# First attention of a two-block transformer kernel: late heads turned in every other pair, compressed branch one pair later

## What is computed

```
q = (rms_norm(to_heads(q, 16), q_gain) * 64 ** -0.5)
kc = rms_norm(compress_blocks(to_heads(kc, g), ...), k_gain[0])      # 15 compressed keys
s_c = einsum(qc, kc) - slopes * dist_c
p_c = masked_softmax(s_c, dist_c >= 0);  o_c = einsum(p_c, vc)
s_s, s_w = scores on the selected and on the window keys;  o_s, o_w = softmax(...) @ v
o = gc[..., 0:1] * o_c + gc[..., 1:2] * o_s + gc[..., 2:3] * o_w
```

## Time and profile before

| | |
|---|---|
| median of 3 runs | 1295.48 us (1290.08 to 1297.04) |
| the profiled execution | 1299.4 us, of which 1297.4 us span |
| TensorE (matmul) busy | 1225.7 us, 94% |
| VectorE busy | 965.9 us, 74% |
| ScalarE busy | 777.4 us, 60% |
| the first attention's loop | about 95 to 169.20 us of the span, where the out-projection's first product starts |
| one weight chunk | 1024.0 KB, 5.3 us from issue to landing |
| mean granted TensorE clock | 0.982 |

### The profile page before, as it was taken

The page is one execution under the profiler, slowest core; times in us unless marked ns, Lnnn a source line. Parts: engine busy times, 40 slices in busy tenths (PEclk is TensorE's granted clock), DMA queues, the critical chain, the costliest instruction groups (busy, mean ns, idle before and its releaser), DMA issues.

```text
span 1297.4 us, 15596 instructions
## 1 busy us (share of the span) xinstructions
PE 1225.7 (94%) x5843; PEld 1000.4 (77%) x5843; DVE 965.9 (74%) x1341; ACT 777.4 (60%) x1155; POOL 20.2 (2%) x36
## 2 busy tenths in 40 slices
PE   7998999999999998999999998999997989999997
PEld 5887777888887786788788776877876867788886
DVE  4978848898987887569989876778786865575545
ACT  6566736677777677557767667433446565543443
POOL 0000000000000000000000000000000001000000
PEclk9998999999999999999999999999999989999999
DMA  7660114798995512429999836777775713467420
GB/s 314 259 240 1 65 66 155 302 367 352 352 364 210 220 58 69 179 103 371 371 344 370 343 106 229 293 310 282 284 306 204 312 61 115 145 279 290 177 98 33
DMA packets 41466, 291.84 MB, mean 225 GB/s; under 512 B 4736, under 2 KB 5120, under 8 KB 6576
## 3 DMA queue, kind: packets, MB, share of 16 engines
q1 hardware_dynamic: 40464, 287.82, 57.9%
q0 software_dynamic: 784, 2.63, 0.7%
q10 hardware_dynamic: 144, 0.39, 0.1%
HBM read 289.78 MB, written 1.05 MB: 224 GB/s over the span
## 4 chain that ended last, share of the span: by engine, by line
PE 67%; DVE 15%; ACT 9%; issue 4%; DMA 4%; POOL 0%; DVEq 0%; ACTq 0%; POOLq 0%
PE ps L422 18%; PE ps L424 18%; PE ps L423 18%; DVE wl L1609 5%; ACT wh L1148 4%; DMA ring<-stream_dram 4%; DVE AR L1833 3%; PE ps L606 2%; ACT AR L1257 1%; PE ps L961 1%; ACT XN L1160 1%; PE ps L559 1%; PE ps L450 1%; PE ps L607 1%; DMA AR<-kr_dram 1%
## 5 line engine op out<-in xcount | busy, mean ns | idle before, releaser
L1609 DVE TENSOR_TENSOR wl<-ring,wh 128x2048 fp32r<-128x2048 f32 x229 | 526.4, 2302 | 165.8 <-ACT wh L1148 162.2
L1148 ACT ACTIVATE wh<-ring 128x2048 fp32r<-128x2048 f32 x232 | 443.8, 1914 | 147.9 <-PE ps L424 80.7
L422 PE MATMUL ps<-wh,XH 128*128 128x512 f32 x1040 | 419.1, 403 | 9.9 <-DVE XH L1653 4.1
L424 PE MATMUL ps<-wh,XL 128*128 128x512 f32 x1040 | 408.1, 392 | 0.0
L423 PE MATMUL ps<-wl,XH 128*128 128x512 f32 x1040 | 407.3, 392 | 0.0
L422 PEld LDWEIGHTS ps<-wh,XH 128*128 128x128 f32 x1040 | 196.9, 189 | 56.5 <-issue 9.9
L424 PEld LDWEIGHTS ps<-wh,XL 128*128 128x128 f32 x1040 | 196.5, 189 | 43.1
L423 PEld LDWEIGHTS ps<-wl,XH 128*128 128x128 f32 x1040 | 197.4, 190 | 38.1 <-issue 0.7
L422 PE MATMUL ps<-wh,HT 128*128 128x512 f32 x360 | 142.6, 396 | 4.0 <-DVE HT L2004 2.9
L424 PE MATMUL ps<-wh,HT 128*128 128x512 f32 x360 | 140.8, 391 | 0.0
L423 PE MATMUL ps<-wl,HT 128*128 128x512 f32 x360 | 140.6, 390 | 0.0
(11 more groups left out here) (299 smaller groups left out, 1255.3 us busy)
## 6 DMA issues: line engine op xcount, KB each, us to landing
ring<-stream_dram SPq DMA_DIRECT2D x272, 1024.0 KB, 5.3
H<-x_dram SPq DMA_DIRECT2D x2, 512.0 KB, 5.0
out_dram<-XN SPq DMA_DIRECT2D x4, 256.0 KB, 2.0
XN<-ag_dram POOLq DMA_DIRECT2D x1, 768.0 KB, 4.5
AR<-pT_dram POOLq DMA_DIRECT2D x2, 256.0 KB, 2.8
AR<-g_final_dram POOLq DMA_DIRECT2D x1, 512.0 KB, 4.8
C<-cols_dram ACTq DMA_DIRECT2D x1, 385.0 KB, 4.7
ring<-stream_dram SPq DMA_DIRECT2D x2, 144.0 KB, 5.2
```

The lines of the kernel that those rows point to most:

```text
L422: e.matmul(o, ah, bh, start=start, stop=False)
L424: return e.matmul(o, al, bh, start=False, stop=stop)
L1148: e.activation(wh[:, k % WBUF, :], ring[:, n % RING, :], ACT.Copy, scale=1.0).then_inc(up("whi", ("whi", k)))
L1609: e.tensor_tensor(wl[:, k % WBUF, :], ring[:, n % RING, :], h.bitcast(F32), ALU.subtract).then_inc(up("wlo", ("wlo", k)))
```

## The change

Of the eight hooks, the late heads move from steps 1, 2, 3, 4 to steps 1, 3, 5, 7 on all three engines; the last two groups go to the banks 0 to 3 of the scores instead of bank 6. The first half of the compressed branch stays in step 0 on TensorE, but in bank 5 and not in the next of 4 and 5; on VectorE it moves from step 0 to step 1, behind the first group of late heads, on ScalarE from step 1 to step 2; its normalising stays in step 2, its turning in step 3. The second half moves from step 6 to step 8, its normalising from 7 to 9, its turning from 8 to 10. The weight splits move from steps 8 and 11 to 6 and 12.

```diff
--- before.py
+++ after.py
@@ -995,7 +995,7 @@
                 project("q1", "mix0", lambda t: [("qsq", 1, t)], between=second_layer)
 
                 def compressed(hf):
-                    b = bank("cs", hf, by=[("cs", hf)], of=(0, 1, 2, 3) if hf else (4, 5))
+                    b = bank("cs", hf, by=[("cs", hf)], of=(0, 1, 2, 3) if hf else (5,))
                     e.wait_ge(*at("kb"))
                     e.wait_ge(*at("lo", ("qt", hf), 6))
                     for t in range(TT):
@@ -1024,13 +1024,13 @@
                     k = [("lo", ("kt", a), j) for a in range(2) for j in (0, 2)] if i == 0 else []
                     return k + ([("lo", ("qt", i // 8), i % 8)] if i % 2 == 0 else [])
 
-                def late_heads(*js):
-                    turn_heads(("qt", 1), QN[:, :, 512:1024], js, [("qn", 1)], (6,))
+                def late_heads(*js, of=(6,)):
+                    turn_heads(("qt", 1), QN[:, :, 512:1024], js, [("qn", 1)], of)
 
                 attention("nsa", nsa_pairs, keys, 0, ready,
-                          {0: lambda: compressed(0), 1: lambda: late_heads(0, 1), 2: lambda: late_heads(2, 3), 3: lambda: late_heads(4, 5),
-                           4: lambda: late_heads(6, 7), 6: lambda: compressed(1)}, closing,
-                          {3: lambda: turn_compressed(0), 8: lambda: turn_compressed(1)})
+                          {0: lambda: compressed(0), 1: lambda: late_heads(0, 1), 3: lambda: late_heads(2, 3), 5: lambda: late_heads(4, 5, of=(0, 1, 2, 3)),
+                           7: lambda: late_heads(6, 7, of=(0, 1, 2, 3)), 8: lambda: compressed(1)}, closing,
+                          {3: lambda: turn_compressed(0), 10: lambda: turn_compressed(1)})
 
             def moba():
                 project_first("skv", "kv", lambda t: [("skvsq", t)], lambda: key_rows(1), (6, 7))
@@ -1478,12 +1478,8 @@
                 def late_heads(*js):
                     high(("qt", 1), js, lambda j: q_of(8 + j), S[:, 8:9])
 
-                def weigh_and_late():
-                    late_heads(0, 1)
-                    weigh(0)
-
-                attention("nsa", nsa_pairs, 0, {1: weigh_and_late, 2: lambda: late_heads(2, 3), 3: lambda: late_heads(4, 5), 4: lambda: late_heads(6, 7),
-                                                6: lambda: weigh(1)}, (8, 11))
+                attention("nsa", nsa_pairs, 0, {1: lambda: late_heads(0, 1), 2: lambda: weigh(0), 3: lambda: late_heads(2, 3), 5: lambda: late_heads(4, 5),
+                                                7: lambda: late_heads(6, 7), 8: lambda: weigh(1)}, (6, 12))
 
             def moba(stage):
                 def query_rows(t):
@@ -2201,24 +2197,20 @@
                     e.wait_ge(*at("pct_full", hf))
                     e.tensor_copy(PCT[:, 256 * hf:256 * hf + 256], ps("pct", hf)[0:120, 0:256]).then_inc(up("dve", ("pct", hf)))
 
-                def first_hook():
-                    q_norm("qn", "qroot", 1)
+                def second_hook():
+                    late_heads(0, 1)
                     e.wait_ge(*at("ct"))
                     compressed(0)
 
-                def third_hook():
+                def fourth_hook():
                     late_heads(2, 3)
-                    normalise(0)
-
-                def fourth_hook():
-                    late_heads(4, 5)
                     turn_compressed(0)
 
                 compressed_keys()
                 q_part(1)
                 attention("nsa", nsa_pairs, 0, True,
-                          {0: first_hook, 1: lambda: late_heads(0, 1), 2: third_hook, 3: fourth_hook, 4: lambda: late_heads(6, 7),
-                           6: lambda: compressed(1), 7: lambda: normalise(1), 8: lambda: turn_compressed(1)}, (8, 11))
+                          {0: lambda: q_norm("qn", "qroot", 1), 1: second_hook, 2: lambda: normalise(0), 3: fourth_hook, 5: lambda: late_heads(4, 5),
+                           7: lambda: late_heads(6, 7), 8: lambda: compressed(1), 9: lambda: normalise(1), 10: lambda: turn_compressed(1)}, (6, 12))
 
             def moba():
                 take()
```

## The result

The changed kernel took 1302.13 us (median of 12 runs, 1298.88 to 1303.26), the kernel before 1295.28 (12 runs on the same chip, 1290.08 to 1297.20). The ratio is 1.0056, with a 95% interval of 1.0045 to 1.0068. So the sign was right and the size was not: +6.85 us, where the sum said +2.7. The profiled execution took 1303.11 us, its span is 1301.1.

What follows compares the result with a forecast made beforehand. TensorE, busy 94% of the span, was taken to bound the kernel, so only its waits count: 1.0 + 2.15 - 0.5 = 2.65, say +2.7, on 1295.48 gives 1298.2 us; range 1293.0 to 1303.0, 8 in 10.

Steps and rivals of the forecast that it cites:

- the sum: Whole kernel: waits of 1.0 and 2.15 us less 0.5 gained, 2.65, taken as +2.7 us; chance 0.40.
- The first term: First pairs, up to pair 5's scores at 117.5 us: TensorE gains 0.5 us after the waits behind it.
- The clock probably falls here too, as behind the 3.8 us. That costs little: First pairs: lower clock near 106 us costs little, as TensorE waits again, up to 2 us for copies, 0.5 for weights.
- the other bound: First pairs: 0.6 us lost instead of 0.5 gained, if the lower clock lasts beyond 111 us.
- The second and third terms: Pairs 8 and 9: TensorE waits 1.0 us for heads 6, 7, then 2.15 us before turning pair 7.
- Rival 1: Pairs 8 and 9: the clock falls in the new stall and all counts, +4.4 us, 1299.9 us; chance 0.32.
- The rest of the kernel moves along: Behind the stage: everything only shifts by the stage's +2.7 us, with no further gain or loss.
- Five microseconds at half rate cost about 2.5: Kernel before, behind the 3.8 us wait before the second late-head group: clock 0.50 until about 111 us costs about 2.5 us.
- rival 2: Pairs 5 to 9 stall under 0.5 us and the clock stays up near 106 us: about -1.5 us, 1294.0; chance 0.16.
- the bound of 0.5%: Whole kernel: a measurement can tell 0.5%, 6.5 us, from no change; chance of staying within it 0.88.
- A slowing by over 6.5 us: Whole kernel: needs rival 1 and a high run, or two falls of the clock; chance 0.09.

Runs made afterwards that it cites:

- second half another pair on: Changed kernel with the second compressed branch in pair 9 and the weight splits in 8 and 12; 1298.45 us, ratio 1.0027.
- 32 transposes: Kernel before plus 32 transposes whose output nothing reads, behind the whole first attention; 1299.13 us, ratio 1.0024.
- second look at before: Kernel before, unchanged, profiled once more for a second trace; 1294.20 us.
- second look at after: Changed kernel, with no further edit, profiled once more for a second trace; 1303.34 us.
- first branch back: Changed kernel with the first compressed branch back in VectorE's step 0 and its weighing in ScalarE's step 1, bank 5 kept; 1299.45 us, ratio 1.0042.
- splits back: Changed kernel with the two weight splits back in pairs 8 and 11; 1298.86 us, ratio 1.0031.
- both back: Changed kernel with the weight splits back in 8 and 11 and the first compressed branch back in steps 0 and 1; 1296.51 us, ratio 1.0015.
- the kernel with later heads: Kernel before with late heads in steps 3, 4, 6, 7, second branch in 8, splits in 9, 12; 1296.32 us; with transposes filling its waits, 1296.57 us.

## Why the prediction was right and wrong, step by step

| step | forecast | measured |
|---|---|---|
| pair 1's maxima | 100.0 | 100.07 |
| branch on VectorE | 104.9 | 104.81 |
| pair 2's maxima | 106.95 | 106.86 |
| turning of pair 0 waits | 0.8 and 2.6 | 0.57 and 2.20 |
| pair 3's scores | 106.3 | 106.14 |
| waits for copies, weights | 2 and 0.5 | 2.10 and 0.44 |
| pair 3's maxima | 111.4 | 111.26 |
| pair 5's scores | 117.5 | 118.72 |
| pair 7's exponentials | 128.5 | 129.60 |
| products wait for heads 6, 7 | 1.0 | 0.69 |
| pair 8's maxima | 134.5 | 135.51 |
| turning of pair 7 waits | 2.15, to 139.7 | 0.24, to 140.97 |
| end of the stage | 171.8 | 172.80 |

**Up to 111.4 us the queues told it to 0.2 us.** Every time in the first pairs is where three queues, followed in strict order with durations of the kernel before, put it; the two waits of pair 0's turning came 0.2 and 0.4 us shorter than forecast.

**The first term, 0.5 us gained, failed.** The step is "The clock probably falls here too, as behind the 3.8 us. That costs little". It did fall, but not with the long waits: it was still at 1.00 in both and fell at 111.3 us, inside the last short wait (0.44 us, to 111.49), when TensorE had two pairs of work in hand. Pair 5's scores came at 118.72, 1.2 us later than forecast. Against before that is a gain of 0.3 us (118.72 less 95.45, and 118.98 less 95.38), with two head groups of 0.44 still to turn: 0.6 us lost. That is the other bound, "if the lower clock lasts beyond 111 us". That the queues were right and the clock was the miss is shown by "second half another pair on": there the fall came at 104.7 us, ahead of the wait for the copies, as the sentence has it, and pair 5's scores stood 22.09 us behind the start of the stage. The forecast, 117.5, is 22.05 behind the start at 95.45.

**The second and third terms were right in sum and wrong in kind.** From pair 5's scores to the end of the stage it took 54.1 us (118.72 to 172.80), and 54.3 were forecast. The heads were late as forecast (0.69 us of 1.0), and the splits and the branch pushed pair 8's maxima to 135.51, 1.0 late like everything behind the first fall. But TensorE came to the turning of pair 7 late as well, because the clock had fallen again at 135.2. From the first turning behind the branch (134.87) to pair 9's scores it took 4.2 us, for some 2.5 at full rate. The 2.15 us of waiting became 1.7 of slow work and 0.24 of waiting. Rival 1 had the fall, but behind the stall, where it would have been added; it came ahead of it and took its place. So the stage missed by what the first fall cost: +3.5 us for +2.7.

**"The rest of the kernel moves along" failed**, and it is the larger part of the miss: 3.3 us of 4.15. It is true of a delay (32 transposes, +3.6 for +3.6). It is not true of this change, which also shifts a counter that hands out banks. The diff shows it in one argument, `(5,)` for `(4, 5)`, which the prediction read only for where the compressed scores lie. 1.6 us of it are two waits with a place; about 1.5 go with the lower mean clock, by the estimate above, and why the clock is lower stays open.

**"Five microseconds at half rate cost about 2.5"** was wrong, and harmless, since the sum did not use it. With the clock kept up the stage was the same to 0.05 us, and with 3.4 us at the lower clock in the place of 6.8, in the second look at before, to 0.02. Behind this wait the other engines were late for the next steps too, and half rate was free; rival 2 had counted on that gain.

**The chances.** The ratio lies a little above the bound of 0.5%, and its interval holds it. The time, 1302.1, is inside the range, near its upper end. That is in part luck: the range reaches so far because of two falls of the clock and the scatter of three runs, and half of the 6.85 us comes from outside the stage, for which the prediction had no term. A slowing by over 6.5 us, which had been given 0.09, is what was measured.

The Trainium skill (TensorE: Matmul & The Clock Gate, HAM oscillation) says that a kernel whose bursts are broken by waits pays for it again and again, since each burst starts slow. The trace agrees in part. The slow work behind 111.3 us was paid for with 1.2 us, that behind 135.2 took the place of a wait, and the bursts behind the gaps of 2.20, 2.10 and 0.69 us all started at 1.00; at 106.24 us, in the kernel before, the burst did start slow and nothing was paid.

## What to carry to other kernels

When a change alters which bank, buffer or slot one step takes from a shared rotation, compare the assignment in the whole program, not only in the stage that is edited: here a parity put a wait of 0.86 us 300 us behind the change, in another layer, and lengthened one by 0.5 us still further on. Ask of a lower clock whether TensorE is the one that is waited for in that stretch before pricing it, and price it at both ends, since a fall can come after the waits, when the work is there, or ahead of one that takes the slow work up. And when one stage's gain or loss does not show in the total, measure a pure delay of the same size first: it tells whether delays or the change itself are at work.

## What the runs showed of the hardware

- The clock can fall after the long gaps. In after it stood at 1.00 through gaps of 2.20 us (to 105.84) and 2.10 us (to 110.21), and fell at 111.3, inside a gap of 0.44 us. In before it fell inside the gap of 3.78 us. The same first pairs had the fall at 104.7 us in "second half another pair on", and 1.2 us less to pair 5's scores.
- A short gap was enough. After a wait of 0.69 us and sixteen products of 30 columns it fell at 135.2, so too in the second look at after and, at 133.8, in "first branch back" (0.66 us). In "splits back" and "both back", with the same sixteen products and no gap ahead of them, it did not.
- Half rate cost nothing from 105 to 111 us in before (stage 73.82 with 6.8 us at the lower clock, 73.84 with 3.4, 73.87 with the clock at 1.00), and 1.4 us in the kernel with later heads (72.39 and 71.00).
- Two executions of the same kernel, with the same stage to 0.02 us, differed by 5.3 us in span. Part of it is the clock (mean 0.982 and 0.989); near 890 us a wait of TensorE for VectorE (L679, L1800) was 1.7 us in the one and 0.5 in the other.
